# Gate-section modulation sums of the first mixer: VectorE multiply-adds in place of column-group matmuls

## The chip, the cores and the metric

One core of a Trainium2 chip runs the whole program in one launch. The metric is the device time of a run in microseconds; lower is better.

## The reference

Two transformer blocks are applied to 256 tokens of width 1024, all in float32. The change touches only the first mixer of the first block, and there only the adaptive modulation:

```python
def ada_terms(cond, w, b):
    return jnp.split(jax.nn.silu(cond) @ w + b, N_ADA, axis=-1)   # w: 1024 x 6144, N_ADA = 6

sh1, sc1, g1, sh2, sc2, g2 = ada_terms(cond_lat, ada_w[i], ada_b[i])
hl = modulate(rmsnorm(x, norm1_g[i]), sh1, sc1)       # h * (1 + scale) + shift
yl = short_conv_mixer(hl, conv_w_in[j], conv_w[j], conv_w_out[j], True)
x = x + g1 * yl
x = x + g2 * swiglu(modulate(rmsnorm(x, norm2_g[i]), sh2, sc2), ffn_w_in[i], ffn_w_out[i])
```

`cond` is one vector of 1024. Each of the six sections is therefore a weighted sum of the 1024 rows of a 1024 x 1024 piece of `ada_w`, plus a bias row. The section in question is `g1`, the gate that multiplies the mixer's output before it is added to `x`.

## The kernel before

The program orders its five engines by semaphores; each engine runs its own list of instructions in the order in which it is written (`pe` is TensorE, `dve` VectorE, `act` ScalarE, `pool` GpSimd, `sp` SyncE).

**Weights.** They come in units of 512 KB twice (128 partitions x 2048 floats), three slots deep. SyncE loads a unit into `raw`, ScalarE writes its rounded half `w_hi` (L1271), VectorE the rest `w_lo` = `raw` - `w_hi` (L1780, the function `split`), and TensorE multiplies with both in three products (`product`, L638 to L640). A slot of `raw` is free again after VectorE's part, a slot of `w_hi` and `w_lo` after TensorE's last use. In the first mixer, units n to n+11 are the input projection (`channel_part`, `channel_unit`), units n+12 to n+15 the output projection (`down_part`), and n+16 is the first unit of the FFN.

**The mixer's own work.** After channel units 4 and 9 VectorE multiplies two sections (`u_out`, L2081), ScalarE makes the middle tap of the convolution (L1556), VectorE the outer taps (L2096), then the product with the third section (`conv_out`, L2104); ScalarE rounds that (L1562) and VectorE writes the rest (`conv_lo`, L2110). All this is done in two halves. The output projection of a half starts when both parts of it are there.

**Modulation sums.** There are three ways of forming them. Shift and scale of the mixer itself come first, by column-group matmuls, and are not touched. The scale of the FFN (SCALE2) and the gate of the mixer (GATE1) go through `mod_piece`: a chunk of 256 rows of `ada_w` is multiplied by `cond32` (the silu of the condition, in the first of 32 columns) in four matmuls that write to four groups of 32 partitions (`column_sums`, L853), pieces 0 to 3 for SCALE2 and 4 to 7 for GATE1. VectorE adds the bias (`section_sum`, L2117), and two matmuls against a selecting column `sel` add the groups and put the row on all partitions (`sum_everywhere`, L881). The chunks of a section land in four buffers, `mod_raw[0..3]`, each reused for GATE1 when the piece of SCALE2 that read it is done (`load_mod`, L526). The shift of the FFN (SHIFT2) goes another way: VectorE multiplies each of eight row tiles of 128 by its column of `cond` and adds it to `ada_acc` (`ada_add`, L2127, two instructions per chunk), GpSimd issues the chunks' loads (L2397), and TensorE sums over the partitions by ones (`shift_columns`, L909).

**The order around the change.** TensorE: channel unit 8, `sum_everywhere(0)`, unit 9, `mod_piece(4)`, units 10 and 11, `mod_piece(5)`, `mod_piece(6)`, then the output projection as parts (unit, token tile): (0,0), (0,1), `mod_piece(7)`, (1,0), (1,1), `sum_everywhere(1)`, (2,0), (3,0), `shift_columns`, (2,1), (3,1), then the FFN. VectorE, from unit 9 on: `u_out(1)`, the split of n+12, `outer_taps(1)`, `ada_add(2)`, the split of n+13, `conv_out(1)`, `conv_lo(1)`, the splits of n+14, `ada_add(3)`, n+15, `section_sum(1)`, n+16. ScalarE copies the spread gate row to `rows` after `sum_everywhere(1)` (L1582); VectorE uses it when part (3,0) is done (L1849). GpSimd, once the mixer's own modulation is done: the loads of SHIFT2 chunks 0 and 1, a memset of `half_sum`, two bias rows to it, then the loads of chunks 2 and 3, each when VectorE has finished with the buffer.

Of the kernel before, what the change touches and what calls it, by code (L numbers as in the profile page):

```python
# [17 lines left out]
ALU = mybir.AluOpType  # L18
# [8 lines left out]
D = 1024  # L27
KT = D // P
# [10 lines left out]
GATE1, SHIFT2, SCALE2, GATE2 = 2, 3, 4, 5  # L39
# [30 lines left out]
HALF = D // 2  # L70
# [60 lines left out]
def block_program(nc, out, **w):  # L131
# [28 lines left out]
    with ExitStack() as ctx:  # L160
        def sb(name, shape, dt=F32):
            return ctx.enter_context(nc.sbuf_tensor(name, shape, dt))

        def sem(name):
            return ctx.enter_context(nc.semaphore(name))

        ps = ctx.enter_context(nc.psum_tensor("ps", [P, 8, 512], F32))
# [10 lines left out]
        act_pair = sb("act_pair", [P, 2 * TOKT, FCH])  # L178
# [6 lines left out]
        ones = sb("ones", [P, P])  # L185
# [5 lines left out]
        cond = sb("cond", [P, KT])  # L191
# [11 lines left out]
        def part(at, *shape):  # L203
            n = 1
            for k in shape:
                n *= k
            assert at + n <= 11776
            ap = arena[:, at:at + n]
            if len(shape) == 1:
                return ap  # L210
            names = "abcd"[:len(shape)]
            return ap.rearrange(f"p ({' '.join(names)}) -> p {' '.join(names)}",
                                **dict(zip(names[1:], shape[1:])))
# [8 lines left out]
        ada_acc = part(6144, D)  # L222
        mod_raw = [ada_v_raw[:, 0, :, :], ada_v_raw[:, 1, :, :], rows[:, 2:4, :], tmp[:, :, :]]
        half_sum = act_pair[:, 0:TOKT, :].rearrange("p t c -> p (t c)")
        scale2_sum = act_pair[:, TOKT:2 * TOKT, :].rearrange("p t c -> p (t c)")
        cond_rows = part(11296, P)[0:KT, :]
        cond32 = part(11424, KT, 32)
# [58 lines left out]
        mod_landed = [sem(f"mod_landed{i}") for i in range(4)]  # L286
        mod_sum_ps = sem("mod_sum_ps")
        mod_sum_sb = sem("mod_sum_sb")
        sum_cleared = sem("sum_cleared")
        sum_bias = sem("sum_bias")  # L290
        cond32_ok = sem("cond32_ok")
        mod_mid = sem("mod_mid")
        xnT_raw = sem("xnT_raw")
# [14 lines left out]
        ada_ps = sem("ada_ps")  # L308
# [103 lines left out]
        def weight_count(n):  # L412

            return n + 1
# [220 lines left out]
        def _(pe):  # L635
# [6 lines left out]
            def unit(n, j=0):  # L642

                pe.wait_ge(raw_done, n + 1 + NSLOT * j)
                return w_hi[:, slot_of(n), :], w_lo[:, slot_of(n), :]

            def tok(t):
                return slice(t * P, (t + 1) * P)
# [182 lines left out]
            def channel_unit(i, bank, u):  # L831

                hi, lo = unit(BASE[CONV] + i)
                for k in range(4):
                    channel_ks(i, bank, u, hi, lo, k)
# [12 lines left out]
            def column_sums(bank, pieces, k0):  # L848

                for j in range(2):  # L850
                    for h in range(2):
                        g = 2 * j + h
                        mm = pe.matmul(ps[32 * g:32 * g + 32, bank, :], cond32[:, k0 + j, :],  # L853
                                       pieces[:, j, h * HALF:(h + 1) * HALF],
                                       start=k0 == 0, stop=k0 == KT - 2, skip_group_check=True)
                return mm
# [16 lines left out]
            def mod_piece(q):  # L873
                pe.wait_ge(mod_landed[q % 4], 16 * (q // 4 + 1))
                column_sums(0, mod_raw[q % 4], 2 * (q % 4)).then_inc(mod_sum_ps, 1)

            def sum_everywhere(i, acc):

                pe.wait_ge(mod_sum_sb, i + 1)
                for h in range(2):  # L880
                    mm = pe.matmul(ps[:, h, :], sel[:, h:h + 1].to_broadcast([P, P]), acc[:, :], start=True, stop=True)  # L881
                mm.then_inc(ada_ps, 1)

            def token_part(n, second, bank, t):

                hi, lo = unit(n)
                for k in range(4):
                    c = slice(k * 512, (k + 1) * 512)
                    kt = 4 * second + k
                    mm = product(ps[:, bank, :], xT_hi[:, kt, tok(t)], xT_lo[:, kt, tok(t)], hi[:, c], lo[:, c],  # L890
                                 kt == 0, kt == KT - 1)
                return mm
# [116 lines left out]
            sum_everywhere(0, scale2_sum)  # L1009
            channel_unit(9, CONV_BANK[4], 1)  # L1010
            pe.wait_ge(ada_row_v, 1)
            mod_piece(4)
            pe.wait_ge(evac_v, 2)
            channel_unit(10, CONV_BANK[5], 0)
            channel_unit(11, CONV_BANK[5], 1)
            mod_piece(5)
            mod_piece(6)
            pe.wait_ge(evac_v, 4)
            pe.wait_ge(evac_a, 2)
            for i, tk in ((0, 0), (0, 1), (1, 0), (1, 1), (2, 0), (3, 0), (2, 1), (3, 1)):  # L1020
                pe.wait_ge(yT_ok, i // 2 + 1)
                mm = down_part(n + 12 + i, yT_hi, yT_lo, 2 * i, tk, i == 0, i == 3)
                if tk:
                    mm.then_inc(w_used, 1)
                elif i == 3:
                    mm.then_inc(y_tok0, 1)
                if (i, tk) == (0, 1):
                    mod_piece(7)
                if (i, tk) == (1, 1):
                    sum_everywhere(1, half_sum)  # L1030
                if (i, tk) == (3, 0):
                    pe.wait_ge(ada_p_part, 2 * ADA_CH)
                    shift_columns(2, ada_acc)
# [35 lines left out]
            for k in range(KT):  # L1069
                c = slice(k * 256 + P, (k + 1) * 256)  # L1070
                mm = product(ps[:, 3, 0:SEQ], hi[:, c], lo[:, c], xT_hi[:, k, :], xT_lo[:, k, :], k == 0, k == KT - 1)
# [114 lines left out]
            for k in range(KT):  # L1186
                mm = product(ps[:, 0, 0:SEQ], zf_hi[:, k, :], zf_lo[:, k, :], xT_hi[:, k, :], xT_lo[:, k, :], k == 0, k == KT - 1)
# [576 lines left out]
        def _(dve):  # L1764
# [8 lines left out]
            def split(n, j=0):  # L1773

                if n >= TOTAL:
                    return
                dve.wait_ge(hi_ready, weight_count(n) + NSLOT * j)
                g = gain_column(n)
                if g is None:
                    dve.tensor_tensor(w_lo[:, slot_of(n), :], raw[:, slot_of(n), :], w_hi[:, slot_of(n), :].bitcast(F32),  # L1780
                                      ALU.subtract).then_inc(raw_done, 1)
                else:
                    for k in range(4):
                        c = slice(k * 512, (k + 1) * 512)
                        o = dve.scalar_tensor_tensor(w_lo[:, slot_of(n), c], raw[:, slot_of(n), c], par[:, g + k:g + k + 1],  # L1785
                                                     w_hi[:, slot_of(n), c].bitcast(F32), ALU.mult, ALU.subtract)
                    o.then_inc(raw_done, 1)
# [319 lines left out]
            def conv_lo(h):  # L2107

                dve.wait_ge(yT_hi_ok, h + 1)
                dve.tensor_tensor(yT_lo[:, 4 * h:4 * h + 4, :], conv_y, yT_hi[:, 4 * h:4 * h + 4, :].bitcast(F32),  # L2110
                                  ALU.subtract).then_inc(yT_ok, 1)

            def section_sum(i, acc):

                dve.wait_ge(sum_bias, 64)
                dve.wait_ge(mod_sum_ps, 4 * i + 4)
                dve.tensor_tensor(acc, ps[:, 0, :], acc, ALU.add).then_inc(mod_sum_sb, 1)  # L2117

            def ada_add(q):

                if q == 0:
                    dve.wait_ge(ada_p_bias, 16)
                dve.wait_ge(ada_p_landed[q % 2], 16 * (q // 2 + 1))
                for i in range(2):
                    k = 2 * q + i
                    dve.wait_ge(ada_p_part, k)
                    o = dve.scalar_tensor_tensor(ada_acc, ada_p_raw[q % 2][:, i, :], cond[:, k:k + 1], ada_acc, ALU.mult, ALU.add)  # L2127
                    o.then_inc(ada_p_part, 1)
# [8 lines left out]
            conv_lo(0)  # L2137
            split(n + 9)
            ada_add(0)
            section_sum(0, scale2_sum)  # L2140
            ada_add(1)
            split(n + 10)
            dve.wait_ge(ada_ps, 1)
# [8 lines left out]
            split(n + 13)  # L2152
            conv_out(1)
            conv_lo(1)
            split(n + 14)
            ada_add(3)
            split(n + 15)
            section_sum(1, half_sum)
            split(n + 16)

            dve.wait_ge(ada_row_v, 1)
# [184 lines left out]
        def _(pool):  # L2346
# [34 lines left out]
            def sum_rows(acc, section):  # L2381
                for h in range(2):
                    pool.dma_start(acc[32 * h:32 * h + 1, :],
                                   w["ada_b"][:, section * D + h * HALF:section * D + (h + 1) * HALF]).then_inc(sum_bias, 16)
# [37 lines left out]
            pool.wait_ge(mod_ps, 4)  # L2422
            load_ada_p(0)
            load_ada_p(1)
            pool.memset(half_sum, 0.0).then_inc(sum_cleared, 1)
            pool.wait_ge(sum_cleared, 2)
            sum_rows(half_sum, GATE1)
            for q in range(2, ADA_CH):
                pool.wait_ge(ada_p_part, 2 * q - 2)
                load_ada_p(q)  # L2430
# [76 lines left out]
```

## Time and profile before

| | us |
|---|---|
| runs of the kernel | 1296.68, 1296.86, 1298.84; median 1296.86 |
| profiled execution: span (no other time of it is recorded) | 1295.4 |
| TensorE busy | 1279.2 (99%) |
| VectorE busy | 866.0 (67%) |
| ScalarE busy | 730.3 (56%) |
| GpSimd busy | 124.6 (10%) |
| mean DMA rate | 195 GB/s, 335 to 402 in the first three fortieths of the span |

The span runs from the first to the last instruction of one profiled execution. "Busy" is the time in which an engine had an instruction at work; matmuls are pipelined and overlap, so the spacing of their starts says more than their durations. An L with a number is a line of the kernel. A bracket behind a row of the timeline is the idle time of that engine just before it and the instruction that ended it. The first mixer runs until about 137 us.

### The profile page before, as it was taken

Reading aid. Unit: us, or ns where it says so; the run is one execution under the profiler, and the core shown is the slowest. Engines: PE = TensorE matmul, PEld = TensorE weight load, DVE = VectorE, ACT = ScalarE, POOL = GpSimd, SP = SyncE. Lnnn points to the kernel's source line nnn. Section 1 sums busy time; section 2 is a strip of 40 time slices with the busy share of each in tenths; the row PEclk is TensorE's granted clock in tenths of the full one; section 3 lists DMA queues with packets and bytes.
Section 4 is the critical chain, followed back from the end, with each engine's and each line's share of the span. In section 5 each row is a group of like instructions: output and inputs, shape, how many; then the busy total and the mean of one; then the engine's idle time right before and its main releaser. Section 6 shows DMA issues by size and latency. Waiting matters only on the chain.

```text
span 1295.4 us, 19942 instructions
## 1 busy us (share of the span) xinstructions
PE 1279.2 (99%) x7343; PEld 1075.1 (83%) x7343; DVE 866.0 (67%) x1157; ACT 730.3 (56%) x1102; POOL 124.6 (10%) x120
## 2 busy tenths in 40 slices
PE   8999999999999999999999999999999999999998
PEld 7887888887888888877888888888887897888886
DVE  4476787555876667586766666766666687766665
ACT  4433644444755556657655557655557556755553
POOL 3000197000640000100000000000000100000000
PEclk9999999999999999999999999999999999999999
DMA  9996486555456565653555554655573543555561
GB/s 335 372 402 218 176 280 205 184 187 179 163 195 194 194 203 170 211 166 98 195 192 182 185 203 150 206 183 182 189 238 102 187 143 111 172 188 191 194 210 65
DMA packets 177125, 252.62 MB, mean 195 GB/s; under 512 B 9336, under 2 KB 143796, under 8 KB 177076
## 3 DMA queue, kind: packets, MB, share of 16 engines
q1 hardware_dynamic: 174080, 243.28, 56.8%
q0 software_dynamic: 2624, 8.48, 1.7%
q8 instruction: 34, 0.56, 0.2%
q10 hardware_dynamic: 372, 0.19, 0.1%
q14 instruction: 15, 0.12, 0.0%
HBM read 248.73 MB, written 1.05 MB: 193 GB/s over the span
## 4 chain that ended last, share of the span: by engine, by line
PE 90%; DVE 4%; ACT 3%; SPq 1%; DMA 1%; issue 1%; DVEq 0%; ACTq 0%
PE ps L745 26%; PE ps L638 14%; PE ps L639 13%; PE ps L640 13%; PE ps L742 13%; PE ps L678 2%; PE ps L686 1%; PE ps L679 1%; PE ps L1085 1%; PE ps L662 1%; DMA raw<-in_conv_w_in 1%; DVE w_lo L1785 1%; DVE w_lo L1780 1%; PE ps L948 1%; SPq L517 1%
## 5 line engine op out<-in xcount | busy, mean ns | idle before, releaser
L745 PE MATMUL ps<-xT_pair,w_hi 128*128 128x512 f32 x1440 | 393.0, 394 | 0.0
L1780 DVE TENSOR_TENSOR w_lo<-raw,w_hi 128x2048 fp32r<-128x2048 f32 x111 | 259.0, 2335 | 99.8 <-ACT w_hi L1271 99.6
L745 PEld LDWEIGHTS ps<-xT_pair,w_hi 128*128 128x128 f32 x1440 | 246.1, 189 | 33.0
L1276 ACT ACTIVATE w_hi<-raw,par 128x512 fp32r<-128x512 f32 x336 | 214.8, 713 | 102.3 <-PE ps L745 101.5
L1271 ACT ACTIVATE w_hi<-raw 128x2048 fp32r<-128x2048 f32 x111 | 211.4, 1906 | 74.5 <-PE ps L640 42.3
L742 PEld LDWEIGHTS ps<-xT_pair,w_lo 128*128 128x128 f32 x1440 | 220.4, 189 | 30.3 <-DVE w_lo L1785 0.3
L1785 DVE SCALAR_TENSOR_TENSOR w_lo<-raw,par,w_hi 128x512 fp32r<-128x512 f32 x336 | 231.4, 750 | 12.8 <-ACT w_hi L1276 12.7
L742 PE MATMUL ps<-xT_pair,w_lo 128*128 128x256 f32 x1440 | 229.3, 281 | 0.1
L638 PE MATMUL ps<-w_lo,hT_hi 128*128 128x512 f32 x400 | 156.9, 392 | 0.0
L639 PE MATMUL ps<-w_hi,hT_hi 128*128 128x512 f32 x400 | 156.1, 390 | 0.0
L640 PE MATMUL ps<-w_hi,hT_lo 128*128 128x512 f32 x400 | 155.7, 389 | 0.0
L1969 DVE TENSOR_TENSOR arena<-ps,arena 128x512 f32<-128x512 f32 x45 | 31.1, 692 | 173.0 <-ACT arena L1431 173.0
L638 PE MATMUL ps<-xT_pair,w_hi 128*128 128x256 f32 x368 | 107.6, 292 | 0.2 <-DVE xT_pair L2035 0.2
L639 PE MATMUL ps<-xT_pair,w_hi 128*128 128x256 f32 x368 | 104.0, 283 | 0.0
L640 PE MATMUL ps<-xT_pair,w_lo 128*128 128x256 f32 x368 | 104.0, 283 | 0.0
L1442 ACT ACTIVATE hT_hi<-act_pair 128x512 fp32r<-128x512 f32 x45 | 28.4, 632 | 111.3 <-PE ps L640 111.3
L638 PEld LDWEIGHTS ps<-w_lo,hT_hi 128*128 128x128 f32 x400 | 75.1, 188 | 16.5 <-issue 0.2
L640 PEld LDWEIGHTS ps<-w_hi,hT_lo 128*128 128x128 f32 x400 | 75.1, 188 | 16.0
L639 PEld LDWEIGHTS ps<-w_hi,hT_hi 128*128 128x128 f32 x400 | 75.1, 188 | 15.7 <-issue 0.2
L638 PEld LDWEIGHTS ps<-xT_pair,w_hi 128*128 128x128 f32 x368 | 70.3, 191 | 13.9 <-issue 11.5
L639 PEld LDWEIGHTS ps<-xT_pair,w_hi 128*128 128x128 f32 x368 | 70.4, 191 | 0.3 <-issue 0.2
L640 PEld LDWEIGHTS ps<-xT_pair,w_lo 128*128 128x128 f32 x368 | 70.4, 191 | 0.0
(290 smaller groups left out, 1628.6 us busy)
## 6 DMA issues: line engine op xcount, KB each, us to landing
raw<-in_ffn_w_gate SPq DMA_DIRECT2D x88, 512.0 KB, 4.0
raw<-in_ffn_w_up SPq DMA_DIRECT2D x88, 512.0 KB, 4.9
raw<-in_ffn_w_down SPq DMA_DIRECT2D x88, 512.0 KB, 4.1
raw<-in_ffn_w_in SPq DMA_DIRECT2D x44, 512.0 KB, 4.7
raw<-in_conv_w_in SPq DMA_DIRECT2D x24, 512.0 KB, 9.6
raw<-in_fox_w_in SPq DMA_DIRECT2D x24, 512.0 KB, 4.5
raw<-in_ffn_w_out SPq DMA_DIRECT2D x22, 512.0 KB, 4.3
raw<-in_ab_w_in SPq DMA_DIRECT2D x14, 512.0 KB, 4.6
```

Of the source, the lines that this page charges most:

```text
L638: pe.matmul(o, a_hi, b_lo, start=first, stop=False, skip_group_check=True)
L639: pe.matmul(o, a_hi, b_hi, start=False, stop=False, skip_group_check=True)
L640: return pe.matmul(o, a_lo, b_hi, start=False, stop=last, skip_group_check=True)
L678: pe.matmul(ps[:, bank, :], x_k, lo[:, c], start=h == 0 and k == 0, stop=False, skip_group_check=True)
L742: pe.matmul(ps[:, bank, 0:SEQ], lo[:, cols[k]], xT_hi[:, 4 * u + k, :], start=u == 0 and k == 0, stop=False, skip_group_check=True)
L745: mm = pe.matmul(ps[:, bank, :].rearrange("p (s c) -> p s c", s=2), hi[:, cols[k]], xT_pair[:, :, 4 * u + k, :], start=False, stop=u == 1 ...
L1271: act.activation(w_hi[:, slot_of(n), :], raw[:, slot_of(n), :], ACT.Copy).then_inc(hi_ready, 1)
L1276: a = act.activation(w_hi[:, slot_of(n), c], raw[:, slot_of(n), c], ACT.Copy, scale=par[:, g + k:g + k + 1])
L1442: act.activation(hT_hi[:, :, :], hid, ACT.Copy).then_inc(hT_hi_ok, 1)
L1780: dve.tensor_tensor(w_lo[:, slot_of(n), :], raw[:, slot_of(n), :], w_hi[:, slot_of(n), :].bitcast(F32), ALU.subtract).then_inc(raw_done, 1)
L1785: o = dve.scalar_tensor_tensor(w_lo[:, slot_of(n), c], raw[:, slot_of(n), c], par[:, g + k:g + k + 1], w_hi[:, slot_of(n), c].bitcast(F32) ...
L1969: dve.tensor_tensor(gate_s, ps[:, 2:4, 0:SEQ], gate_rest, ALU.add).then_inc(gate_sum, 1)
```

## The change

TensorE loses the four pieces of GATE1. VectorE gets `gate_add(q)`: for each of the four chunks, two multiply-adds of 128x1024 onto `gate_acc`, of the form that `ada_add` has, placed after `conv_lo(1)`, after the split of n+14, after `ada_add(3)` and after the split of n+15. `section_sum(1)` goes. In place of `sum_everywhere(1)` stands `gate_everywhere()`: it waits for all eight adds and multiplies `gate_acc` by a 128x128 matrix of ones, once for each half of the row. `gate_acc` takes all of `act_pair`, of which the second half held `scale2_sum`; so GpSimd waits for the first spreading (`ada_ps` at 1) before it clears it, and one bias row is loaded in place of two. What GpSimd has behind that, the loads of SHIFT2 chunks 2 and 3, comes after it. The loads of the GATE1 chunks are issued as before.

```diff
+        gate_acc = act_pair[:, :, :].rearrange("p t c -> p (t c)")
...
+            def gate_everywhere():
+
+                pe.wait_ge(gate_part, KT)
+                for h in range(2):
+                    mm = pe.matmul(ps[:, h, :], ones[:, :], gate_acc[:, h * HALF:(h + 1) * HALF], start=True, stop=True)
+                mm.then_inc(ada_ps, 1)
...
             channel_unit(9, CONV_BANK[4], 1)
             pe.wait_ge(ada_row_v, 1)
-            mod_piece(4)
             pe.wait_ge(evac_v, 2)
             channel_unit(10, CONV_BANK[5], 0)
             channel_unit(11, CONV_BANK[5], 1)
-            mod_piece(5)
-            mod_piece(6)
...
-                if (i, tk) == (0, 1):
-                    mod_piece(7)
                 if (i, tk) == (1, 1):
-                    sum_everywhere(1, half_sum)
+                    gate_everywhere()
...
+            def gate_add(q):
+
+                if q == 0:
+                    dve.wait_ge(gate_bias, 16)
+                dve.wait_ge(mod_landed[q], 32)
+                for i in range(2):
+                    k = 2 * q + i
+                    dve.wait_ge(gate_part, k)
+                    dve.scalar_tensor_tensor(gate_acc, mod_raw[q][:, i, :], cond[:, k:k + 1], gate_acc, ALU.mult, ALU.add).then_inc(gate_part, 1)
...
             conv_out(1)
             conv_lo(1)
+            gate_add(0)
             split(n + 14)
+            gate_add(1)
             ada_add(3)
+            gate_add(2)
             split(n + 15)
-            section_sum(1, half_sum)
+            gate_add(3)
             split(n + 16)
...
             load_ada_p(0)
             load_ada_p(1)
-            pool.memset(half_sum, 0.0).then_inc(sum_cleared, 1)
+            pool.wait_ge(ada_ps, 1)
+            pool.memset(gate_acc, 0.0).then_inc(sum_cleared, 1)
             pool.wait_ge(sum_cleared, 2)
-            sum_rows(half_sum, GATE1)
+            pool.dma_start(gate_acc[0:1, :], w["ada_b"][:, GATE1 * D:(GATE1 + 1) * D]).then_inc(gate_bias, 16)
             for q in range(2, ADA_CH):
                 pool.wait_ge(ada_p_part, 2 * q - 2)
                 load_ada_p(q)
```

## Rows read from the trace of the kernel before

**Rows 1.** The page: span, busy time of each engine, and the chain's shares.

```profile
span 1295.4 us, 19942 instructions
...
PE 1279.2 (99%) x7343; PEld 1075.1 (83%) x7343; DVE 866.0 (67%) x1157; ACT 730.3 (56%) x1102; POOL 124.6 (10%) x120
...
PE 90%; DVE 4%; ACT 3%; SPq 1%; DMA 1%; issue 1%; DVEq 0%; ACTq 0%
```

**Rows 2.** The chain in order of time: start, length, engine, line.

```profile
94.02 1.30 DVE arena L2081 x2
...
115.99 1.00 PE ps L853 x8
```

**Rows 3.** Timeline of TensorE: start, duration, line, operation, shapes, count, idle before.

```profile
86.35 1.88 PE L881 MATMUL ps<-act_pair,arena 128*128 128x512 f32 x4
...
93.91 1.07 PE L853 MATMUL ps<-arena 128*32 128x512 f32 x8
...
107.49 1.04 PE L853 MATMUL ps<-rows,arena 128*32 128x512 f32 x8
110.25 0.50 PE L638 MATMUL ps<-w_lo,yT_hi 128*128 128x512 f32 x1 [1.72 <-DVE arena L2104]
...
122.49 1.88 PE L881 MATMUL ps<-act_pair,arena 128*128 128x512 f32 x4
```

**Rows 4.** Timeline of VectorE, 103 to 125 us.

```profile
104.27 2.60 DVE L2127 SCALAR_TENSOR_TENSOR arena<-arena,cond 128x1024 f32<-128x1024 f32 x2
106.78 2.28 DVE L1780 TENSOR_TENSOR w_lo<-raw,w_hi 128x2048 fp32r<-128x2048 f32 x1
108.98 1.22 DVE L2104 TENSOR_TENSOR arena<-ps,arena 128x1024 f32<-128x1024 f32 x1
111.33 1.23 DVE L2110 TENSOR_TENSOR yT_lo<-arena,yT_hi 128x1024 fp32r<-128x1024 f32 x1 [1.13 <-ACT yT_hi L1562]
```

**Rows 5.** Timeline of ScalarE: unit n+15.

```profile
116.08 1.91 ACT L1271 ACTIVATE w_hi<-raw 128x2048 fp32r<-128x2048 f32 x1 [2.99 <-PE ps L640]
```

**Rows 6.** Stretches: length; PE, PEld, DVE, ACT, POOL busy; granted clock, DMA share, GB/s.

```profile
105.00:107.00 2.00, 2.00 (x19) 1.63 (x21) 1.97 (x3) 0.00 (x0) 0.00 (x0) 1.00 0.92 265
107.00:109.00 2.00, 1.53 (x16) 0.26 (x8) 2.00 (x2) 0.00 (x0) 0.00 (x0) 1.00 0.07 8
109.00:111.00 2.00, 0.75 (x3) 0.66 (x4) 1.20 (x2) 0.77 (x1) 0.00 (x0) 1.00 0.30 60
...
1290.00:1291.00 1.00, 0.00 (x0) 0.00 (x0) 0.99 (x3) 0.95 (x3) 0.00 (x0) 1.00 0.55 207
...
1293.00:1294.00 1.00, 0.00 (x0) 0.00 (x0) 0.00 (x0) 0.00 (x0) 0.00 (x0) 0.50 0.88 326
```

**Rows 7.** Timeline of TensorE, first 30 us: passes on `ones`, early and later.

```profile
3.60 7.12 PE L669 MATMUL ps<-ones 128*128 128x128 f32 x36
...
16.24 2.48 PE L669 MATMUL ps<-ones 128*128 128x128 f32 x20
```

**Rows 8.** Timeline of GpSimd: a clear of 128x1024, and the issue of SHIFT2 chunk 2.

```profile
29.14 0.95 POOL L2416 MEMSET arena<- 128x1024 f32 x1 [17.54 <-PE ps L870]
...
83.17 0.74 POOL L2397 DMA_DIRECT2D arena<-in_ada_w  x1 [26.37 <-DVE arena L2127]
```

**Rows 9.** DMA issues, 60 to 140 us: count, KB each, median us to landing.

```profile
raw<-in_ffn_w_in SPq DMA_DIRECT2D x8, 512.0 KB, 4.5
rows<-in_ada_w SPq DMA_DIRECT2D x1, 1024.0 KB, 15.1
arena<-in_ada_w POOLq DMA_DIRECT2D x1, 1024.0 KB, 9.9
xn<-in_ada_w POOLq DMA_DIRECT2D x1, 1024.0 KB, 11.8
```

**Rows 10.** What TensorE waited for in the whole span: total, times, longest.

```profile
PE ps L638 <- DVE arena L2104: 1.7, 1, 1.7
...
PE ps L678 <- ACT xT_pair L1329: 0.9, 1, 0.9
```

More of the change, by code:

```diff
@@ L290, in block_program @@
         sum_bias = sem("sum_bias")
+        gate_bias = sem("gate_bias")
+        gate_part = sem("gate_part")
         cond32_ok = sem("cond32_ok")
@@ L2111, in conv_lo, with section_sum @@
                                   ALU.subtract).then_inc(yT_ok, 1)
[L2113 to L2117, printed above, removed]
+            def section_sum():
+                dve.wait_ge(sum_bias, 32)
+                dve.wait_ge(mod_sum_ps, 4)
+                dve.tensor_tensor(scale2_sum, ps[:, 0, :], scale2_sum, ALU.add).then_inc(mod_sum_sb, 1)
+            def gate_add(q):
[6 more added lines that the diff above has]
+                    dve.scalar_tensor_tensor(gate_acc, mod_raw[q][:, i, :], cond[:, k:k + 1], gate_acc, ALU.mult, ALU.add).then_inc(gate_part, 1)
             def ada_add(q):
@@ L2139, in _ @@
             ada_add(0)
-            section_sum(0, scale2_sum)
+            section_sum()
             ada_add(1)
```

## The prediction

> **What bounds the kernel now.** The page first [rows 1]: TensorE is busy for 1279.2 of 1295.4 us and VectorE for 67%, so time is gained by issuing less on TensorE and lost by anything that makes it wait. The chain that ended last says the same: 90% of it is TensorE [rows 1]. An average doesn't tell about the first mixer, so I then read the chain there in order of time [rows 2]. Three stretches are to be seen. Up to about 94 us the chain runs on TensorE. From 94.02 to 110.2 us it runs on VectorE and ScalarE (evacuation, middle taps, weight split, outer taps, shift-section adds, weight split, product by the gate), while TensorE only has the last two channel units and must then wait. From 110.25 us on it is TensorE again, without a gap: output-projection parts, one column-group piece, the two matmuls that spread the gate row, more parts. So an instruction taken off TensorE counts only in the first and third stretch, and one put on VectorE counts in the second, or where TensorE comes to wait for it.
>
> The timeline of TensorE [rows 3] places the four pieces of the gate section. Piece 4 is at 93.91 us, piece 5 and then piece 6 (107.49) follow unit 11, all three ahead of the wait of 1.72 us that VectorE's L2104 ends at 110.25 us. Piece 7 is at 115.99 us in the chain [rows 2], within the third stretch.
>
> **What is removed on TensorE.** A piece is eight overlapped passes and takes 1.00 us of the chain [rows 2]. Pieces 4, 5 and 6 are worth nothing: the first projection part can't start before L2104, whose predecessors on VectorE start from the end of channel unit 9, before piece 4. TensorE just reaches that wait about 3 us earlier: 1.7 becomes 4.6 to 4.7 us. Piece 7 is worth 1.0 us of path. The two spreading matmuls stay two fp32 matmuls of 128x512, four passes with a 128x128 operand, 1.88 us from 122.49 on [rows 3]; the operand `ones` instead of `sel` costs nothing. So TensorE would be through the fourth projection part at 122.49 - 1.0 = 121.5 us.
>
> **What is added on VectorE.** Eight multiply-adds of 128x1024, of the form of `ada_add` (same opcode, same shapes, scalar by column). A pair of these takes 2.60 us, and the next instruction starts 2.51 us after the pair's start (104.27 to 106.78); a weight split follows on after 2.20 us (106.78 to 108.98) [rows 4]. What goes is one sum of 128x512, L2117, which lay in VectorE's idle time. No add is placed ahead of L2110 (`conv_lo(1)`), so VectorE's second stretch is unchanged up to there: L2110 starts at 111.33 and lets the next start at 112.5 (111.33 + 1.23, less the 0.08 by which neighbours overlap) [rows 4]. The queue is in order, and until the last gate add it now holds five pairs (four of the gate, `ada_add(3)`) and the splits of units n+14 and n+15:
>
> 112.5 + 5 x 2.51 + 2 x 2.20 = 112.5 + 12.55 + 4.40 = 129.45 us start to start, about 129.55 us to the end of the last.
>
> No other input of these is late. ScalarE's half of n+14 comes right after its L1562, that of n+15 is ready at 118.0 us [rows 5]; the splits now start at 115.0 and 124.8. The four chunks of weights are issued where they were, after pieces 0 to 3, which stay; the last, to `tmp`, needed at 127 us, was used by TensorE at 115.99 already [rows 2]. The bias row has from 90 to 112 us.
>
> **The new wait.** `gate_everywhere` stands in TensorE's order after the fourth projection part, and waits for all eight adds. TensorE comes to it at 121.5 us and goes on at 129.6 (the 0.05 us after VectorE as at 110.25 [rows 3, 4]): an idle time of 8.1 us. Queued behind it are the projection parts (2,0), (3,0), `shift_columns`, (2,1), (3,1), and after them all of the FFN. The first of these need only the splits of n+14 (done at 117.3) and n+15 (done at 127.1), so they'd be ready sooner, but can't pass. Net shift of everything from the spreading matmuls on: 129.6 - 122.5 = 7.1 us (8.1 of wait less 1.0 of piece 7). Seen from VectorE: its adds are 10.0 us, and it had 1.9 us free between 112.6 and 121.5.
>
> **TensorE's clock.** The granted clock is 1.00 of full speed (2.4 GHz) in every slice of the page but falls once: from 1290 us there is no matmul, the clock still reads 1.00 up to 1291, and in the stretch from 1293 it reads 0.50 (1.2 GHz) [rows 6]. The idle of 1.72 us at 108.5 left it at 1.00 [rows 6]. An idle of 8.1 us is well beyond what preceded that fall, so I expect 1.2 GHz when the spreading matmuls start. What the return costs is bounded from below by nothing (0) and by the start of the kernel from above: there 36 passes on `ones`, after 3.4 us without work, took 7.12 us, and 20 of the same later 2.48 us [rows 7]; 36 at that pace are 4.46 us, so the slow phase cost 2.7 us (the granted clock column says 1.00 there, but the durations show the lower level). I take 2.7, since that row is the nearest thing: the same engine restarted after idling, with dense work. The first idle (now 4.6 us) may do the same to the projection parts from 110.25 us on; that is covered by the 8.1 us wait, which would be shortened to 5.4 us and cost nothing.
>
> [...]
>
> **GpSimd and the queues.** GpSimd now waits for the first spreading (from 86.35 us, done at about 88.1 [rows 3]) before it clears the accumulator (0.95 us for 128x1024 [rows 8]) and issues the bias and then chunks 2 and 3 of the shift section. Chunk 2 was issued at 83.17 [rows 8] and will be at about 89.9, chunk 3 behind it. Chunk 2 is needed by VectorE at 104.27 us. The two chunks landed 9.9 and 11.8 us after issue [rows 9]; 89.9 + 11.8 = 101.7, or 102.4 if the 0.7 us of the issue itself is counted: hidden by some 2 us. The cover is thin, as the DMA engines are full until about 106 us [rows 6]: with the 15.1 us of the slowest such load [rows 9] it would be there at 105.0 to 105.7, 0.7 to 1.4 us late, and they stand still from 107 [rows 6], which bounds the loss at about 3 us. And every microsecond that VectorE loses there now moves its adds, and so the end. I take 0. The memset beside VectorE's L2145 (88 to 89.5 us) costs from 0 to its own 0.95 us, covered by the 2.3 us that VectorE idled before 94.02. SyncE's loads for n+17, n+18 and n+19 wait for splits that come 2, 7 and 5 us later; they take 4.5 us [rows 9] and are used after 141 us: nothing. ScalarE's copy of the gate row waits for the spreading (to about 133 us, if that goes at half speed), but its user starts after part (3,0), at 136.9 or later: nothing.
>
> **The sum.** -1.0 (piece 7) + 8.1 (wait) + 2.7 (clock) = +9.8 us. Downstream nothing gives it back: in the remaining 1150 us TensorE waits for others 0.9 us at most at once, and each of those waits follows from its own results [rows 10]. The span goes from 1295.4 to 1305.2 us. Of the profiled execution only the span is recorded; the median of the three runs, 1296.86, is 1.5 above it. With the same offset: 1306.7 us.
>
> **The rivals.**
> - *Wait without clock cost.* TensorE waits 8.1 us but the clock returns at once or never falls. For it: the 1.72 us idle that left it alone; against it: the fall at 1293. +7.1: 1304.0 us.
> - *The shift chunk comes late.* Chunk 2 lands after 104.27 us, VectorE's whole order slides. For it: full DMA engines; against it: 2 us of cover. +9.8 and 1 to 3: 1307.7 to 1309.7 us.
> - *The adds are hidden (faster).* VectorE has the sum ready before TensorE asks at 121.5 us; then only piece 7 is seen, 1295.9 us. It decides where eight adds fit in the 1.9 us that VectorE had free, 0.24 us each. The rows say 1.28 [rows 4], and the last one stands behind two splits. Almost nothing for it.
> - *The stage after gives it back.* The FFN's start would have to hold 7 us or more of waits that don't move with TensorE. The list of waits has none [rows 10]. About 1297 us.
>
> **How the numbers follow.** Forecast 0.68, wait without clock cost 0.15, late chunk 0.11, given back 0.03, hidden 0.03. The unknown sizes: clock 1.2 to 3.5 (a restart may meet a shorter or longer slow phase than the start did), about 0.5 for the wait. So the forecast's own range is 1304.9 to 1308.0; with the neighbours it is 1303.4 to 1309.4. About 0.2% (2.6 us) is what a measurement of this kernel can tell from no change. Slower by more than that: the first three, 0.94. Within: 0.03. Faster by more needs 2.6 us, which even the hidden case doesn't give; I leave 0.03 for what I don't see, from that case's share.
>
> **What would show it.** In the trace after: VectorE without a gap from about 112.5 to 129.5 us, ten multiply-adds of 1.28 us between L2110 and the split of n+16; one idle of about 8 us of TensorE before the two matmuls on `gate_acc`, released by VectorE's add, and one of 4 to 5 us before the first projection part; the granted clock at 0.50 in or after the first of these, and matmuls of the spreading and of part (2,0) at twice their duration; the same durations as before from about 138 us on, all of it 9 to 10 us later. The forecast is wrong if the clock reads 1.00 throughout and the durations are unchanged (then 1304), if VectorE waits before `ada_add(2)` (then more), or if TensorE's wait before `gate_everywhere` is below 6 us although the clock stayed up.

## The result, and the profile after

The changed kernel is slower: median 1306.10 us of 4 runs (1305.00 to 1307.85) against 1296.98 us of 4 runs (1296.68 to 1298.84), ratio 1.0064 with a 95% interval of 1.0049 to 1.0078. (The ratios in this document are estimated over all runs and aren't the quotient of the medians, which is 1.0070 here. In the experiments below each ratio is to 27 runs of the kernel before made beside them, with medians of 1297.43, 1297.08 and 1297.02.) The prediction was 1306.7 us. The profiled run took 1306.0 us with a span of 1304.2, 8.8 above the span before.

Line numbers of the changed kernel are higher by 3 at the products (L641 for L638), by 10 at `shift_columns` (L919), by 5 to 15 on VectorE and by 18 to 28 on GpSimd; L891 is `gate_everywhere`, L2132 `gate_add`. In the experiments they differ by one or a few again. The page again, for [rows 1]:

```profile
span 1304.2 us, 19886 instructions
...
PE 1279.0 (98%) x7311; PEld 1076.1 (83%) x7311; DVE 874.9 (67%) x1164; ACT 730.6 (56%) x1102; POOL 124.5 (10%) x119
...
PE 89%; DVE 4%; ACT 3%; issue 1%; SPq 1%; DMA 1%; DVEq 0%; ACTq 0%
```

TensorE has 32 passes less and is busy for the same time: two slow phases, shown below, have stretched what remains. VectorE has 8.9 us more. Timeline of TensorE, for [rows 3], with what stands around both of its idle times:

```profile
110.34 0.80 PE L641 MATMUL ps<-w_lo,yT_hi 128*128 128x512 f32 x1 [4.76 <-DVE arena L2109]
110.94 0.63 PE L642 MATMUL ps<-w_hi,yT_hi 128*128 128x512 f32 x1
...
116.69 0.40 PE L641 MATMUL ps<-w_lo,yT_hi 128*128 128x512 f32 x1
...
129.68 3.78 PE L891 MATMUL ps<-act_pair,ones 128*128 128x512 f32 x4 [5.31 <-DVE act_pair L2132]
132.47 1.28 PE L641 MATMUL ps<-w_lo,yT_hi 128*128 128x512 f32 x1
...
138.85 1.84 PE L919 MATMUL ps<-ones,arena 128*128 128x1 f32 x16
```

The wait before the first projection part is 4.76 us in place of 1.72; the one before the spreading matmuls, 5.31 us, is new; the spreading starts at 129.68 us (122.49 before) and takes 3.78 us in place of 1.88. VectorE in the same stretch, for [rows 4]:

```profile
104.35 2.60 DVE L2142 SCALAR_TENSOR_TENSOR arena<-arena,cond 128x1024 f32<-128x1024 f32 x2
...
111.41 1.23 DVE L2115 TENSOR_TENSOR yT_lo<-arena,yT_hi 128x1024 fp32r<-128x1024 f32 x1 [1.12 <-ACT yT_hi L1567]
112.56 2.60 DVE L2132 SCALAR_TENSOR_TENSOR act_pair<-arena,cond,act_pair 128x1024 f32<-128x1024 f32 x2
115.07 2.28 DVE L1785 TENSOR_TENSOR w_lo<-raw,w_hi 128x2048 fp32r<-128x2048 f32 x1
...
127.02 2.60 DVE L2132 SCALAR_TENSOR_TENSOR act_pair<-tmp,cond,act_pair 128x1024 f32<-128x1024 f32 x2
129.54 2.28 DVE L1785 TENSOR_TENSOR w_lo<-raw,w_hi 128x2048 fp32r<-128x2048 f32 x1
```

No row from 112.56 to 129.54 us has a bracket: VectorE has no idle time there, and the last add ends at 129.62, 0.06 before TensorE goes on. The stretches, columns as in [rows 6]: the clock falls in the first idle time, is back by 117, falls again in the second, and is back by 134. (1.00 is 2.4 GHz and 0.50 is 1.2 GHz; a value between them is a slice in which the clock changed.)

```profile
108.00:109.00 1.00, 0.00 (x0) 0.00 (x0) 1.00 (x1) 0.00 (x0) 0.00 (x0) 1.00 0.05 4
109.00:110.00 1.00, 0.00 (x0) 0.00 (x0) 1.00 (x2) 0.00 (x0) 0.00 (x0) 0.79 0.00 0
110.00:111.00 1.00, 0.66 (x2) 0.56 (x3) 0.29 (x1) 0.68 (x1) 0.00 (x0) 0.50 0.52 132
...
116.00:117.00 1.00, 1.00 (x5) 0.78 (x4) 1.00 (x1) 0.00 (x0) 0.00 (x0) 0.80 0.00 0
117.00:118.00 1.00, 1.00 (x6) 0.82 (x5) 1.00 (x2) 0.00 (x0) 0.00 (x0) 1.00 0.00 0
...
126.00:127.00 1.00, 0.00 (x0) 0.00 (x0) 1.00 (x1) 0.38 (x1) 0.00 (x0) 0.82 0.00 0
127.00:128.00 1.00, 0.00 (x0) 0.00 (x0) 1.00 (x2) 0.00 (x0) 0.00 (x0) 0.50 0.00 0
...
134.00:135.00 1.00, 1.00 (x6) 0.78 (x6) 0.00 (x0) 0.52 (x1) 0.00 (x0) 1.00 1.05 313
```

GpSimd, for [rows 8], and where its chunks landed, for [rows 9]: chunk 2 was issued at 90.14 and was there 11.2 us later, at 101.3, 3 us ahead of its use at 104.35.

```profile
88.38 0.95 POOL L2444 MEMSET act_pair<- 128x1024 f32 x1 [33.34 <-PE ps L884]
...
90.14 0.72 POOL L2415 DMA_DIRECT2D arena<-in_ada_w  x1
```

```profile
arena<-in_ada_w POOLq DMA_DIRECT2D x1, 1024.0 KB, 11.2
```

TensorE's waits, for [rows 10], have two entries where there was one of 1.7 us:

```profile
PE ps L891 <- DVE act_pair L2132: 5.3, 1, 5.3
PE ps L641 <- DVE arena L2109: 4.8, 1, 4.8
```

Almost nothing is given back: the transposes at the start of later stages, which were at 144.05, 520.61 and 986.35 us, are at 153.23, 529.78 and 995.50, all 9.15 to 9.18 later. At the end of the program the difference is 8.8. The 0.36 us between lies in one place: the kernel before has, at 1033.76 us, a short wait of TensorE for VectorE, and the changed kernel doesn't have it.

```profile
PE ps L937 <- DVE xn L2203: 0.3, 1, 0.3
```

The traces of all seven experiments on the changed kernel lack it too, and those of the four on the kernel before have it. What removes it isn't shown.

### The profile page after: what moved, and what is told of

Read it like the earlier page. It is cut to its first block, busy times and chain, and to the rows that moved or that the text cites. A ratio compares the mean times of both kernels' runs of the same rounds, so it can differ in the third digit from the quotient of the medians.

```text
span 1304.2 us, 19886 instructions
## 1 busy us (share of the span) xinstructions
PE 1279.0 (98%) x7311; PEld 1076.1 (83%) x7311; DVE 874.9 (67%) x1164; ACT 730.6 (56%) x1102; POOL 124.5 (10%) x119
## 4 chain that ended last, share of the span: by engine, by line
PE 89%; DVE 4%; ACT 3%; issue 1%; SPq 1%; DMA 1%; DVEq 0%; ACTq 0%
PE ps L748 25%; PE ps L641 14%; PE ps L642 13%; PE ps L643 13%; PE ps L745 13%; PE ps L681 2%; PE ps L689 1%; PE ps L682 1%; PE ps L1090 1%; PE ps L665 1%; DVE w_lo L1790 1%; DMA raw<-in_conv_w_in 1%; SPq L520 1%; DVE act_pair L2132 1%; PE ps L958 1%
## 5 line engine op out<-in xcount | busy, mean ns | idle before, releaser
L641 PE MATMUL ps<-w_lo,hT_hi 128*128 128x512 f32 x400 | 156.9, 392 | 0.0
L641 PE MATMUL ps<-xT_pair,w_hi 128*128 128x256 f32 x368 | 107.5, 292 | 0.2 <-DVE xT_pair L2040 0.2
L641 PEld LDWEIGHTS ps<-w_lo,hT_hi 128*128 128x128 f32 x400 | 75.1, 188 | 16.5 <-issue 0.2
L641 PEld LDWEIGHTS ps<-xT_pair,w_hi 128*128 128x128 f32 x368 | 70.3, 191 | 13.1 <-issue 10.6
```

Source lines behind the costliest of these rows:

```text
L641: pe.matmul(o, a_hi, b_lo, start=first, stop=False, skip_group_check=True)
```

## The experiments

The theory in all of them: TensorE waits in a fixed place of its order for a sum that stands at the end of VectorE's full queue, and each idle time of that length costs it its clock as well. To test the clock, some runs fill an idle time with dummy matmuls: `keep_warm(n)` multiplies `ones` by `ones` n times, 128x128, two passes each, and nobody uses what comes out. As the start-up shifts single profiled runs by up to 2.2 us, times within the mixer are compared from the start of the first projection part (110.25 us before, 110.34 after).

**Ask later.**

```diff
-                if (i, tk) == (1, 1):
-                    gate_everywhere()
                 if (i, tk) == (3, 0):
+                    gate_everywhere()
```

> The changed kernel with gate_everywhere moved in TensorE's order from behind part (1,1) to behind part (3,0), ahead of shift_columns; everything else the same, VectorE's adds included. Theory (the loss is TensorE's wait in a fixed place, plus the clock it costs): TensorE reaches the new place at about 129.8 us (its parts still start at 1.2 GHz at 110.3), the adds are ready at 129.6, so there is no idle above 0.5 us there and no second fall of the clock; the mixer ends 1.5 to 2.8 us later than in the kernel before, span 1297 to 1298.5 us, 6 to 7 us below the changed kernel. Rival (the added 10 us of VectorE's work push the end, wherever TensorE asks for them): span stays within 1 us of 1304.

Measured: 1300.28 us (11 runs) against 1297.43 before, ratio 1.0021 (1.0012 to 1.0030). Of the 9.1 us some 6.3 are gone with all of VectorE's adds still there, so the rival falls: it isn't the work but the place where it is waited for. What is left, +2.85, is just above the range that I gave from the mixer alone (in its profiled run the first part starts 2.2 us late, hence a span of 1300.3). The trace names the rest: the parts still start slow (1.6 us in this trace), part (3,0) now waits 1.4 us for the split of n+15 behind the adds, and the later gate row delays the residual and with it an FFN matmul by 1.2 us; less 1.2 us for piece 7, which two runs below measure, that is 3.0.

```profile
PE ps L641 <- DVE w_lo L1784: 1.4, 1, 1.4
PE ps L689 <- DVE xT_pair L1896: 1.2, 1, 1.2
```

**Keep TensorE warm in the second wait.**

```diff
                 if (i, tk) == (1, 1):
+                    keep_warm(24)
                     gate_everywhere()
```

> The changed kernel with 24 dummy matmuls of 128x128 on ones (48 passes) put into TensorE's order just before it waits for the adds of the gate. At full speed they fill about 5.1 of the 5.3 us. Theory: the wait ends at the same time (the spreading starts at 129.6 to 129.8 us), but the clock stays at 1.00, the spreading takes 1.9 us in place of 3.8, and everything after it is 2.0 us earlier: span 1302.2 (1301.8 to 1302.7). Rival (the slow spreading has another cause, its operand or its place): still 3.8 us, span 1304 to 1305.

Measured: span 1302.2, median 1303.93 (ratio 1.0046, 1.0032 to 1.0059). The timeline of TensorE: the spreading starts at the same time and is fast. So 2.0 us of the loss by the spans (1.9 within the mixer) are the clock, and nothing but that idle time made the spreading slow.

```profile
124.11 5.52 PE L672 MATMUL ps<-ones 128*128 128x128 f32 x48
129.59 1.98 PE L891 MATMUL ps<-act_pair,ones 128*128 128x512 f32 x4
```

The stretch in which the spreading starts, where the changed kernel reads 0.50:

```profile
129.00:130.00 1.00, 1.00 (x7) 0.73 (x6) 1.00 (x2) 0.00 (x0) 0.00 (x0) 1.00 0.98 308
```

**Half the adds.**

```diff
-            gate_add(0)
...
-            gate_add(1)
...
-                pe.wait_ge(gate_part, KT)
+                pe.wait_ge(gate_part, 4)
```

> The changed kernel with the adds of the first two gate chunks left out (that half of the gate's sum is missing). Theory: VectorE has the rest ready at about 125.7 us in place of 129.6, TensorE comes at 124.2, so its idle is about 1.5 us and the clock doesn't fall a second time: gain 3.9 + 2.0, span about 1298.3 (1297.5 to 1299). Rival (what is lost is a fixed cost of the wait, not VectorE's queue): gain under 1 us.

Measured: span 1297.7, median 1299.91 (1.0015, 1.0006 to 1.0024), 6.2 us below the changed kernel. TensorE waits 1.76 us, and the spreading is fast behind it:

```profile
125.06 1.99 PE L891 MATMUL ps<-act_pair,ones 128*128 128x512 f32 x4 [1.76 <-DVE act_pair L2132]
```

**TensorE's part alone, in the kernel before: the pieces ahead of the wait, and the one behind it.** In the first run pieces 4 to 6 are deleted, in the second 20 dummy matmuls stand in their place, in the third piece 7 alone is deleted.

```diff
-            mod_piece(4)
...
             channel_unit(11, CONV_BANK[5], 1)
-            mod_piece(5)
-            mod_piece(6)
```

```diff
             channel_unit(11, CONV_BANK[5], 1)
-            mod_piece(5)
-            mod_piece(6)
+            keep_warm(20, bank=1)
```

```diff
-                if (i, tk) == (0, 1):
-                    mod_piece(7)
```

> The kernel before, with the column-group pieces 4, 5 and 6 left out and nothing put in their place (those parts of the gate's sum are missing). TensorE has 3 us less to do ahead of its wait for conv_out(1). Theory: the wait ends at the same 110.3 us, the idle grows from 1.7 to about 4.7 us, the clock falls, and the projection parts run at 1.2 GHz for some 6 us on the path: the kernel gets slower by 2 to 3 us although work is taken out, span 1297.4 to 1298.4. Rival 1 (removed work ahead of a wait is worth nothing): 1295.4. Rival 2 (it is worth its 3 us): 1292.4.

> The kernel before without pieces 4, 5 and 6, as in the run e4_no_456 (those parts of the gate's sum are missing), but with 20 dummy matmuls (about 4.3 us) after channel unit 11. Theory: with TensorE kept at work the clock stays at 1.00 and the loss of e4_no_456 is gone: span 1295.4 within 0.6, 2 to 3 us below e4_no_456. Rival (e4's loss, if any, comes from the missing pieces in another way): as e4_no_456.

> The kernel before with column-group piece 7 left out (its part of the gate's sum is missing), the only piece that stands behind the wait for conv_out(1). Theory: part (1,0) follows part (0,1) at once, and all from there on is 1.0 us earlier, the second residual included: span 1294.4 (1294.1 to 1294.7). Rival (VectorE's queue holds the hand-over here too): 1295.4.

Measured, in that order: 1299.44 us (1.0015, 1.0006 to 1.0025); 1297.39 (1.0003, 0.9994 to 1.0012); 1295.86 (0.9991, 0.9982 to 1.0000). TensorE's timelines of the three, in one fence each:

```profile
109.78 0.79 PE L638 MATMUL ps<-w_lo,yT_hi 128*128 128x512 f32 x1 [4.76 <-DVE arena L2101]
...
124.15 1.88 PE L881 MATMUL ps<-act_pair,arena 128*128 128x512 f32 x4
```

```profile
104.84 4.63 PE L669 MATMUL ps<-ones 128*128 128x128 f32 x40
109.76 0.50 PE L638 MATMUL ps<-w_lo,yT_hi 128*128 128x512 f32 x1 [0.29 <-DVE arena L2102]
...
122.00 1.88 PE L881 MATMUL ps<-act_pair,arena 128*128 128x512 f32 x4
```

```profile
110.04 0.50 PE L638 MATMUL ps<-w_lo,yT_hi 128*128 128x512 f32 x1 [1.74 <-DVE arena L2102]
...
121.06 1.88 PE L881 MATMUL ps<-act_pair,arena 128*128 128x512 f32 x4
```

From the first part to the spreading the kernel before takes 122.49 - 110.25 = 12.24 us. Without pieces 4 to 6 it takes 14.37: three microseconds of work taken out cost 2.1. With dummies in their place it is 12.24 again. Without piece 7 it is 11.02, so this piece is worth 1.22 us, not the 1.00 that the chain gives it: at its two seams the matmuls of the kernel before start 0.32 and 0.34 us after their neighbours, where elsewhere in these parts they follow after 0.23, and that goes too. Its medians, 1295.86 against 1297.02, are at the edge of what the runs can tell (the interval ends at 1.0000), but the trace carries the gain to the end of the program: the last matmul is 1.45 us earlier, of which 0.21 is the start-up. So the recorded rival falls.

**Keep TensorE warm in the first wait only.** In the changed kernel:

```diff
             channel_unit(11, CONV_BANK[5], 1)
+            keep_warm(20, bank=1)
```

> The changed kernel with 20 dummy matmuls (40 passes, about 4.3 us) after channel unit 11, in TensorE's first idle. Theory (the first fall of the clock is covered by the second wait): the clock stays at 1.00 at 110.3, TensorE comes to gate_everywhere at 121.5 to 121.7 us in place of 124.3 and then idles 8 us in place of 5.3; the spreading starts at 129.7 as before and still runs slow, so the span stays at 1304.2 within 0.6 (a longer idle before the restart may make the slow phase longer, by 1 us at most). Rival (both falls count in full): 1301.7.

Measured: span 1304.1, median 1305.95 (1.0067, 1.0052 to 1.0083). The first fall is gone and the time is the same; the second wait has taken it up:

```profile
110.20 0.50 PE L641 MATMUL ps<-w_lo,yT_hi 128*128 128x512 f32 x1 [0.29 <-DVE arena L2110]
129.54 3.78 PE L891 MATMUL ps<-act_pair,ones 128*128 128x512 f32 x4 [8.17 <-DVE act_pair L2133]
```

**GpSimd's part alone.** In the kernel before:

```diff
+            pool.wait_ge(ada_ps, 1)
             pool.memset(half_sum, 0.0).then_inc(sum_cleared, 1)
...
-                dve.wait_ge(sum_bias, 64)
+                dve.wait_ge(sum_bias, 32 * (i + 1))
```

> The kernel before with GpSimd's part of the change alone: it waits for the first spreading before it clears the gate's accumulator, so the loads of shift chunks 2 and 3 are issued at about 90 and 91 us in place of 83.2 and 86.3 (VectorE's first section sum waits for its own two bias rows only). Theory: chunk 2 lands at 101 to 102 us, ahead of its use at 104.3; nothing moves, span 1295.4 within 0.6. Rival (late chunk): VectorE idles before ada_add(2), and the span grows by that idle.

Measured: 1296.99 against 1297.08 (1.0002, 0.9993 to 1.0012), span 1295.1. The late loads cost nothing.

**A better order.** Three versions of the changed kernel with all of its sums. The first:

```diff
             u_out(1)
+            gate_add(0)
             split(n + 12)
...
             conv_lo(1)
-            gate_add(0)
             split(n + 14)
             gate_add(1)
-            ada_add(3)
-            gate_add(2)
             split(n + 15)
+            gate_add(2)
             gate_add(3)
+            ada_add(3)
             split(n + 16)
...
             channel_unit(11, CONV_BANK[5], 1)
+            keep_warm(20, bank=1)
...
                 if (i, tk) == (3, 0):
+                    gate_everywhere()
+                if (i, tk) == (2, 1):
                     pe.wait_ge(ada_p_part, 2 * ADA_CH)
                     shift_columns(2, ada_acc)
```

The second and third have this in TensorE's order instead, and the third also this in VectorE's:

```diff
                 if (i, tk) == (3, 0):
+                    gate_everywhere()
                     pe.wait_ge(ada_p_part, 2 * ADA_CH)
                     shift_columns(2, ada_acc)
```

```diff
-            split(n + 16)
...
                 residual(b, 0)
                 if b == CONV:
+                    split(BASE[CONV] + 16)
```

> The changed kernel, all of its sums, with three things moved: VectorE's gate_add(0) behind u_out(1), where it idled 3.6 us, and its splits of n+14 and n+15 ahead of the other adds, ada_add(3) last; TensorE's gate_everywhere behind part (3,0) and shift_columns behind (2,1); 20 dummy matmuls in TensorE's first idle. Theory: the gate sum is ready at 125 us and asked for at 127, the shift sum ready at 127.7 and asked for at 131.4, both idles of TensorE are filled or gone and the clock stays up; the mixer ends 1.0 to 1.2 us earlier than in the kernel before (piece 7 gone): span 1294.2 to 1294.6, 10 us below the changed kernel. Rival (the later gate row or shift row holds the hand-over to the FFN): 1295.5 to 1298.

> The run e8_reordered with one thing moved back: shift_columns right behind gate_everywhere, ahead of part (2,1). In e8 its result came to ScalarE's queue at 133.0 us, ahead of the square of the new x, and VectorE idled 2.05 us in place of 1.60 before the reciprocal. Theory (the hand-over to the FFN hangs on VectorE's chain, which starts when its full queue ends at 130.1 us): the 0.6 us of ScalarE's queue is gone, the chain is as in the kernel before, 0.1 us later, and the 1 us that TensorE gained is idle time in the hand-over: span 1295.4 within 0.3 after the start-up is taken off. Rival (ScalarE's order was all that held it): 1294.4.

> The run e10_shift_early with VectorE's split of unit n+16 moved behind the first residual, into its idle time before the reciprocal. Theory: the residual starts when the gate row is in place, at 129.6 to 129.7 us in place of 130.1, and all after it is 0.4 us earlier: span 1294.9 to 1295.2, which the runs can't tell from the kernel before; the trace can. Rival (the split was not what held the residual): as e10.

Measured: 1297.39 us (1.0000, 0.9991 to 1.0009), 1296.84 (0.9997, 0.9987 to 1.0006) and 1296.94 (0.9998, 0.9989 to 1.0007). The reorder takes back the whole loss of the change, but the gain of 1.0 that I expected of the first isn't there; the rival put on record with it, 1295.5 to 1298 us, came true (span 1295.6). Its TensorE gets all sums without an idle time and then waits in the hand-over to the FFN (residual, normalisation, transposes and evacuation of the new `x`, from VectorE to ScalarE and back), and so it does in the second, whose timelines of VectorE and TensorE show why:

```profile
127.80 2.29 DVE L1785 TENSOR_TENSOR w_lo<-raw,w_hi 128x2048 fp32r<-128x2048 f32 x1
130.00 1.22 DVE L1854 TENSOR_TENSOR tmp<-ps,rows 128x1024 f32<-128x1024 f32 x1
```

```profile
126.52 1.88 PE L891 MATMUL ps<-act_pair,ones 128*128 128x512 f32 x4
...
141.09 1.17 PE L689 MATMUL ps<-w_hi,xT_pair 128*128 128x512 f32 x4 [1.32 <-DVE xT_pair L1897]
```

The residual could start with the gate row, which ScalarE has copied by 129.45 us, but VectorE's queue holds it until 130.00, as late as in the kernel before; TensorE's gain is the 1.32 us in the bracket. The third version moves the split at 127.80 into the idle time behind the residual. The residual does start 0.4 us earlier (against the first part), but the split is longer than that idle time (2.29 against 1.6), and the reciprocal behind it comes 24.2 us after the first part, as in the second (24.1). My expectation of 0.4 us was wrong. So none of these is measurably faster than the kernel before. In that kernel VectorE idles 3.0 us before the residual, so the gain of e12_no_7 gets through; in e10_shift_early the adds have used that idle time up.

## Why the prediction was right

- *The first three pieces are worth nothing.* Right, and the runs say more: less than nothing, taken alone. Deleting them costs 2.1 us (e4_no_456) through the clock, which dummies give back (e7_no_456_warm). I had priced this fall and put it under the later wait; e6_warm_first shows that it lay there in full (8.17 us of wait without it, 5.31 with it).
- *Piece 7, -1.0.* It measured -1.22 (e12_no_7). The chain's row gives the piece itself and not the seams.
- *The wait, +8.1.* Without the first fall of the clock it is 8.17 us. The last add ended at 129.62 against 129.55 forecast, from a sum of ten adds and two splits. Net shift of the spreading: 129.68 - 122.49 = 7.19, forecast 7.1.
- *The clock, +2.7.* The mechanism was right, the size too large. `shift_columns` was at 129.69 and is at 138.85: 9.16, less 7.19, is 1.97; e2_warm_gate takes away 2.0. The term rested on one start-up row (36 passes in 7.12 us). In the changed kernel the same 36 passes took 6.07 us, a cost of 1.6 by the same sum, and in the thirteen profiled runs of this document they took 5.69 to 7.15 us, a cost of 1.2 to 2.7: the prediction had met one of the slowest start-ups.

```profile
3.40 6.07 PE L672 MATMUL ps<-ones 128*128 128x128 f32 x36
```

- *Wait without clock cost.* This rival is out: both waits end with an instruction of VectorE, TensorE has no matmul meanwhile, and the clock reads 0.50 in both.
- *The late chunk.* It had 3 us of cover in the changed kernel, and GpSimd's part alone moves nothing (e5_pool_only).
- *The adds are hidden, the later stage gives it back.* Neither, but for 0.36 us: the list of waits had one of 0.3 us (L937) that does give way, which the prediction ruled out. But asking at a later place hides most of them (e1_ask_later), which the prediction did not price as the remedy it is.

The sum was -1.0 + 8.1 + 2.7 = 9.8; the trace has 7.2 (wait less piece 7) + 2.0 = 9.2 at the end of the mixer, and the medians differ by 9.1. The order and the mechanism are as forecast. That the median came within 0.6 us has some luck in it: the span was forecast 1.0 too high (1305.2 against 1304.2: the clock 0.7 and the later wait 0.36), and the offset from span to median, taken as 1.5, was 1.9.

## What to carry to other kernels

When work moves from a full engine to one that looks idle, count the queue of the receiving engine from its last free moment to the point at which the first one asks; the busy share of 67% said nothing, ten adds and two splits between that moment and the ask said all. Where the asking engine's order is fixed, move the question first: here that alone took back 6.3 of 9.1 us. And before taking small matmuls out of a stretch that ends in a wait, look whether they are what keeps the clock up; a few dummies in their place cost nothing here (12.24 us with them as before).

## What the runs showed of the hardware

Idle times of 1.4 to 1.8 us left TensorE's granted clock at 1.00 in every trace. Those of 4.8 to 8.2 us took it to 0.50 (1.2 GHz) each time. Inside the mixer no idle time between 1.8 and 4.7 us was met. What one fall cost in the matmuls behind it was not one number, nor set by the length of the idle time. The second fall cost 2.0 us behind 5.31 us of idle time in the changed kernel and about as much behind 8.17 in e6_warm_first. The first one stands behind 4.75 or 4.76 us of idle time in five traces. From the start of the first projection part to that of the fourth e6_warm_first, without the fall, takes 8.29 us; the changed kernel and e2_warm_gate take 11.14, e3_half_adds 10.32, e1_ask_later 9.88. In e4_no_456, with piece 7 between, it is 11.65 against 9.52 in the kernel before. So the same idle time cost 2.9, 2.9, 2.0, 1.6 and 2.1 us. The cost goes with the time for which TensorE worked before the clock came back: in the changed kernel it restarts at 110.34 us and the clock returns in the stretch from 116, in e4_no_456 it restarts at 109.78 and the clock returns in that from 114:

```profile
108.00:109.00 1.00, 0.00 (x0) 0.00 (x0) 1.00 (x2) 0.00 (x0) 0.00 (x0) 0.50 0.08 7
...
114.00:115.00 1.00, 1.00 (x5) 0.79 (x5) 1.00 (x2) 0.00 (x0) 0.00 (x0) 0.80 0.00 0
```

If the clock changed once within each such slice, that is work at 0.50 for about 6.1 and 4.6 us (an estimate from the readings of 0.80), and the cost is a little under half of it in both. What decides when it returns is not shown here. In e1_ask_later the clock still read 1.00 until TensorE had restarted, 4.75 us after it went idle, and fell then:

```profile
111.00:112.00 1.00, 0.00 (x0) 0.00 (x0) 1.00 (x2) 0.00 (x0) 0.00 (x0) 1.00 0.08 17
112.00:113.00 1.00, 0.52 (x2) 0.47 (x3) 0.42 (x1) 0.54 (x1) 0.00 (x0) 0.90 0.42 105
113.00:114.00 1.00, 1.00 (x4) 0.81 (x3) 0.45 (x1) 1.00 (x2) 0.00 (x0) 0.50 1.06 307
```

So a fall can come after the work is back, and a single trace gives its cost only to within about 1.3 us. During the start-up the granted clock reads 1.00 though the passes on `ones` take about twice their time: in the kernel before they start 0.21 us apart until about 9.5 us and 0.11 us apart from then on. There the spacing is to be read, not that column.
